# The gate vectors of the second block: two transfers through DRAM in place of products with the identity

## The chip, the cores and the metric

The kernel runs on one core of a Trainium2 chip, as one launch. The metric is the device time in microseconds (us), from the start to the end of the execution. The core has TensorE (PE), VectorE (DVE), ScalarE (ACT), GpSimd (POOL), and SyncE (SP), which here issues most of the DMA transfers, and 16 DMA engines.

## The reference, cut to what matters

Two blocks of two layers each run one after the other on 256 tokens of width 1024. The change concerns the second block only. There each layer has a modulation vector of 6 x 1024 numbers per stream (the latent tokens and the context tokens), and two of the six parts are gates. A gate multiplies, column by column, what a mixer or an MLP gives back, before the sum and the norm:

```python
for i in range(DEPTH):
    mod = (silu_c @ ada_w[i] + ada_b[i])[:, None, :]
    mod_c = silu_cc @ ada_w[i] + ada_b[i]
    sh1, sc1, g1, sh2, sc2, g2 = jnp.split(mod, 6, axis=-1)
    sh1c, sc1c, g1c, sh2c, sc2c, g2c = jnp.split(mod_c, 6, axis=-1)
    h = x * (1.0 + sc1) + sh1
    ...                                  # y = retention (layer 0) or neighbourhood attention (layer 1)
    x = layer_norm_2(DN_ALPHA * x + g1 * y, ln_g[i, 0], ln_b[i, 0])
    h = x * (1.0 + sc2) + sh2
    x = layer_norm_2(DN_ALPHA * x + g2 * sq_relu_mlp(h, mlp_w1[i], mlp_w2[i]), ln_g[i, 1], ln_b[i, 1])
    if not last:
        ctx = layer_norm_2(DN_ALPHA * ctx + g1c * yc, ln_g[i, 0], ln_b[i, 0])
        ...                              # the same MLP for ctx, with g2c
```

So six gate vectors of 1024 numbers are used: g1, g1c, g2, g2c of layer 0, and g1, g2 of layer 1.

## The kernel before

All five engines have programs written out by hand, each in its own order; they meet only at semaphores. `Lane` counts what each engine gives and takes.

**Weights.** SP fetches each weight unit (128 x 2048 numbers, two transfers of 512 KB) into one of four `raw` slots. ACT copies a unit to `w_hi` in a shorter form (L419, two halves), DVE subtracts it from `raw` and leaves the rest in `w_lo` (L426, two halves), and PE makes each product out of three: hi by hi, hi by lo, lo by hi (L444, L445, L446). There are two `w_hi`/`w_lo` slots. ACT may fill a slot again only when PE has begun on the next unit (semaphore `w_used`), so at each new unit of PE the chain is PE, ACT L419, DVE L426, and then PE two units on.

**Stages in time.** The first block ends with its feed-forward layer; its down part takes some 5.5 us of PE a unit and ends at 791 us. A layer norm follows (POOL makes the power -0.5, L1077 and L1080). Then the retention mixer (to 1200 us), the MLP of layer 0 with 512 tokens (`mlp4`, 1235 to 1600 us), the attention mixer (to 1830 us) and the MLP of layer 1 with 256 tokens (`mlp2`, 1844 to 2020 us). After each norm of the second block POOL applies gain and bias to the tokens that are kept (`pool_stream`, L1973 and L1976: products and sums of two tensors in SBUF), while PE already works on the first MLP units.

**Gates.** `mod` holds the modulation with the column number spread over the 128 partitions. The gate is wanted along the free dimension and equal in all partitions (`gate_b`, two streams by 1024). `pe_gates` makes this out of products: for each group of 128 columns the gate's column, repeated 128 times, by the identity, into banks 4 to 7; `act_gates` copies the banks to `gate_b`. It runs at four places: in the down part of the last feed-forward layer of the first block (two streams), behind the first unit of `mlp4` (two), behind the second of the eight query and key units of the attention mixer (one), and behind the first unit of `mlp2` (one). A product on full float32 shows as two records in the trace. DVE reads `gate_b` only at the end of each of the four stages. `up_by_stream` and `up` are PE's units of the up part; from the third unit on they wait for `hh`, that is for DVE's `hh_lo` (L2402).

Of the kernel before, what the change touches and what calls it, by code (L numbers as in the profile page):

```python
# [215 lines left out]
def build(nc, a, out):  # L216

    with ExitStack() as ctx:
# [10 lines left out]

        sb = tensors(ctx)  # L230
# [686 lines left out]
        def pe_ffn(pe, l):  # L917
# [9 lines left out]
            for j in range(FT // 2 - (2 if l + 1 < DEPTH else 1)):  # L927
# [3 lines left out]
                if j == 2:  # L931
                    pe.eng.wait_ge(on("conv_f"), pe.takes("conv_f", 2))
                    if l + 1 == DEPTH:
                        pe.eng.wait_ge(on("coef"), pe.takes("coef"))
                        pe_gates(pe, 0, 2, (0, 1))
                if j == 4 and l + 1 == DEPTH:
                    pe_gates_end(pe, (0, 1))
# [338 lines left out]
        def act_ffn(act, l):  # L1276
# [25 lines left out]
            for n in range(FT // 2):  # L1302
                if n + (2 if l + 1 < DEPTH else 1) < FT // 2:
                    split_hi(act)
                if l + 1 == DEPTH:
                    if n == 3:
                        act.eng.wait_ge(on("coef"), act.takes("coef"))
                        act_gates(act, (0, 1))
# [512 lines left out]
        def pe_gates_end(pe, streams):  # L1821

            pe.eng.wait_ge(on("gate_b"), pe.takes("gate_b", 2 * len(streams)))
# [346 lines left out]
        def dve_head(dve, h, last_head):  # L2170
# [53 lines left out]
            if last_head:  # L2224
                dve.eng.wait_ge(on("y_add"), dve.given("y_add"))
                dve.eng.wait_ge(on("xc_in"), dve.takes("xc_in", 16))
                dve.eng.wait_ge(on("gate_b"), dve.takes("gate_b", 4))
# [83 lines left out]
        def pe_mlp(pe, l, tiles):  # L2311
# [24 lines left out]
            def step(what, b, c):  # L2336
# [4 lines left out]
                for j in range(2):  # L2341
                    if what == "up":
                        if j == 0 and pe.loop is None and c == 0:
# [4 lines left out]
                            pe_gates(pe, l, 5, streams)  # L2348
# [6 lines left out]
                if what == "up" and pe.loop is None and c == 0:  # L2355
                    pe_gates_end(pe, streams)
# [3 lines left out]
        def act_mlp(act, tiles):  # L2360
# [3 lines left out]
            def step(what, b, c):  # L2364
                for j in range(2):
# [12 lines left out]
                    if what == "up" and j == 0 and act.loop is None and c == 0:  # L2378
                        act_gates(act, streams)
# [4 lines left out]
        def dve_mlp(dve, tiles):  # L2384
# [3 lines left out]
            def step(what, b, c):  # L2388
                if c is last_down:
                    return  # L2390
                for j in range(2):
# [13 lines left out]
                    else:  # L2405
# [3 lines left out]
                        if j == 0 and dve.loop is None:  # L2409
                            dve.eng.wait_ge(on("y_add"), dve.given("y_add"))  # L2410
                            dve.eng.wait_ge(on("gate_b"), dve.takes("gate_b", 2 * len(streams)))
# [94 lines left out]
        def pe_nat(pe):  # L2506
# [6 lines left out]
            for f in range(NF):  # L2513
# [5 lines left out]
                if f == 1:  # L2519
                    pe.eng.wait_ge(on("nv"), pe.takes("nv", 4))  # L2520
                    pe_gates(pe, 1, 2, (0,))
            pe_gates_end(pe, (0,))
# [65 lines left out]
        def act_nat(act):  # L2588
# [9 lines left out]
            for f in range(NF):  # L2598
# [5 lines left out]
                if f == 1:  # L2604
                    act_gates(act, (0,))
# [277 lines left out]
```

## Time and profile before

| | |
|---|---|
| Median of 3 runs | 2032.34 us (2031.33 to 2033.85) |
| Profiled execution, its own time | 2037.13 us |
| Its span, first to last instruction | 2035.2 us |
| PE busy | 1971.5 us, 97% of the span |
| DVE busy | 1254.9 us, 62% |
| ACT busy | 864.2 us, 42% |
| POOL busy | 174.4 us, 9% |
| Mean DMA rate | 146 GB/s |
| Mean granted TensorE clock | 0.993 of full speed |

The profiled execution took 4.79 us more than the median of the runs shown, of which 1.93 us lie outside the span. Times in the rows are counted from the start of the span. A row of the timeline is one group of equal instructions: its start, its busy time, engine, line, and in square brackets the idle time of the engine before it and what ended that.

### The profile page before, as it was taken

The page shows a single profiled execution, that of the slowest core. Times are in us where ns is not written, and L with a number is a line of the kernel's source. Part 1 is how long each engine was busy: PE and PEld are TensorE (multiplying, and loading weights), DVE is VectorE, ACT ScalarE, POOL GpSimd, SP SyncE. Part 2 cuts the span into 40 slices and gives each one's busy share as a digit, 9 for nine tenths or more (in the row PEclk, how much of TensorE's full clock was granted, in tenths as well). Part 3 has the DMA queues.
Part 4 walks back from the last instruction along what each step waited for, and adds up shares of the span by engine and source line. Part 5 has one row for each costly group of instructions (what it writes and reads, how often), then busy time and mean ns, then how long its engine had stood idle before and what let it go on. Part 6 is the DMA issues. An engine that isn't in the chain of part 4 may idle for free.

```text
span 2035.2 us, 32477 instructions
## 1 busy us (share of the span) xinstructions
PE 1971.5 (97%) x12673; PEld 1615.6 (79%) x12673; DVE 1254.9 (62%) x2071; ACT 864.2 (42%) x1445; POOL 174.4 (9%) x175
## 2 busy tenths in 40 slices
PE   9998999999899999999999999999999999999997
PEld 8766999797569988777777777888888787667996
DVE  6666787576568856544545477444445833866667
ACT  5442665354336646232222225223222433855442
POOL 2012000001010001000000005000000330303000
PEclk9999999999999999999999999999999999999999
DMA  8489665465977645222322222323323262545662
GB/s 252 166 311 294 182 186 190 145 187 180 339 222 212 193 178 179 83 83 62 95 70 82 70 76 87 100 89 97 100 86 103 84 141 97 86 103 161 201 186 83
DMA packets 327160, 297.25 MB, mean 146 GB/s; under 512 B 35030, under 2 KB 248354, under 8 KB 327056
## 3 DMA queue, kind: packets, MB, share of 16 engines
q1 hardware_dynamic: 322960, 283.22, 46.0%
q0 software_dynamic: 4096, 12.58, 1.9%
q8 instruction: 74, 1.21, 0.2%
q14 instruction: 30, 0.25, 0.0%
HBM read 294.70 MB, written 1.05 MB: 145 GB/s over the span
## 4 chain that ended last, share of the span: by engine, by line
PE 82%; DVE 10%; DMA 3%; ACT 2%; issue 2%; POOL 1%; SPq 1%; DVEq 0%; ACTq 0%; POOLq 0%
PE ps L444 24%; PE ps L446 24%; PE ps L445 24%; DVE w_lo L426 2%; PE ps L2088 2%; DMA raw<-in_ada_w 2%; PE ps L595 1%; DVE npr L2664 1%; PE ps L2533 1%; PE ps L2069 1%; DVE small L1866 1%; PE ps L1817 1%; ACT w_hi L419 1%; PE ps L489 1%; DMA raw<-in_w_in 0%
## 5 line engine op out<-in xcount | busy, mean ns | idle before, releaser
L426 DVE TENSOR_TENSOR w_lo<-raw,w_hi 128x1024 fp32r<-128x1024 f32 x428 | 526.0, 1270 | 333.6 <-ACT w_hi L419 333.3
L419 ACT ACTIVATE w_hi<-raw 128x1024 fp32r<-128x1024 f32 x428 | 428.9, 1052 | 532.0 <-PE ps L444 444.9
L444 PE MATMUL ps<-zt_hi,w_hi 128*128 128x512 f32 (+1 forms) x816 | 275.0, 337 | 5.0 <-issue 1.4
L446 PE MATMUL ps<-zt_hi,w_lo 128*128 128x512 f32 (+1 forms) x816 | 274.1, 336 | 0.0
L445 PE MATMUL ps<-zt_lo,w_hi 128*128 128x512 f32 (+1 forms) x816 | 274.0, 336 | 0.0
L444 PE MATMUL ps<-xt_hi,w_hi 128*128 128x256 f32 x864 | 241.6, 280 | 1.9 <-DVE w_lo L426 1.8
L446 PE MATMUL ps<-xt_hi,w_lo 128*128 128x256 f32 x864 | 241.1, 279 | 0.0
L445 PE MATMUL ps<-xt_lo,w_hi 128*128 128x256 f32 x864 | 241.0, 279 | 0.0
L444 PEld LDWEIGHTS ps<-zt_hi,w_hi 128*128 128x128 f32 x816 | 153.9, 189 | 25.1 <-issue 3.5
L445 PEld LDWEIGHTS ps<-zt_lo,w_hi 128*128 128x128 f32 x816 | 154.1, 189 | 18.3
L446 PEld LDWEIGHTS ps<-zt_hi,w_lo 128*128 128x128 f32 x816 | 154.1, 189 | 18.2
L444 PEld LDWEIGHTS ps<-xt_hi,w_hi 128*128 128x128 f32 x864 | 164.5, 190 | 2.3 <-DVE w_lo L426 2.3
L445 PEld LDWEIGHTS ps<-xt_lo,w_hi 128*128 128x128 f32 x864 | 163.1, 189 | 0.0
L446 PEld LDWEIGHTS ps<-xt_hi,w_lo 128*128 128x128 f32 x864 | 162.9, 189 | 0.0
L444 PE MATMUL ps<-w_hi,hh_hi 128*128 128x512 f32 x384 | 150.8, 393 | 0.8 <-DVE w_lo L426 0.8
L445 PE MATMUL ps<-w_lo,hh_hi 128*128 128x512 f32 x384 | 151.3, 394 | 0.0
L446 PE MATMUL ps<-w_hi,hh_lo 128*128 128x512 f32 x384 | 150.7, 393 | 0.0
L444 PE MATMUL ps<-w_hi,zt_hi 128*128 128x512 f32 x320 | 127.1, 397 | 1.3 <-DVE w_lo L426 1.2
L446 PE MATMUL ps<-w_hi,zt_lo 128*128 128x512 f32 x320 | 126.0, 394 | 0.0
L445 PE MATMUL ps<-w_lo,zt_hi 128*128 128x512 f32 x320 | 125.6, 392 | 0.0
L2000 DVE TENSOR_TENSOR y<-y,ps 128x512 f32<-128x512 f32 x108 | 72.1, 684 | 86.0 <-PE ps L446 86.0
L1694 DVE SCALAR_TENSOR_TENSOR hid<-ps,par,hid 128x254 f32<-128x254 f32 (+1 forms) x176 | 76.8, 478 | 40.2 <-ACT hid L1281 34.2
(388 smaller groups left out, 3322.9 us busy)
## 6 DMA issues: line engine op xcount, KB each, us to landing
raw<-in_mlp_w SPq DMA_DIRECT2D x128, 512.0 KB, 4.4
raw<-in_ada_w SPq DMA_DIRECT2D x96, 512.0 KB, 7.0
raw<-in_w_up SPq DMA_DIRECT2D x88, 512.0 KB, 5.0
raw<-in_w_in SPq DMA_DIRECT2D x56, 512.0 KB, 4.8
raw<-in_ret_w_in SPq DMA_DIRECT2D x48, 512.0 KB, 4.2
raw<-in_w_down SPq DMA_DIRECT2D x44, 512.0 KB, 4.2
raw<-in_nat_w_in SPq DMA_DIRECT2D x24, 512.0 KB, 5.0
raw<-in_w_out SPq DMA_DIRECT2D x16, 512.0 KB, 7.1
```

The lines of the kernel that those rows point to most:

```text
L419: nc.scalar.activation(w_hi[:, t, w], raw[:, s, w], ACT.Copy).then_inc(on("w_hi"), act.gives("w_hi"))
L426: nc.vector.tensor_tensor(w_lo[:, t, w], raw[:, s, w], w_hi[:, t, w].bitcast(F32), ALU.subtract).then_inc(on("w_split"), dve.gives("w_split"))
L444: first = nc.tensor.matmul(out_ap, l_hi, r_hi, start=start, stop=False)
L445: nc.tensor.matmul(out_ap, l_hi, r_lo, start=False, stop=False)
L446: return first, nc.tensor.matmul(out_ap, l_lo, r_hi, start=False, stop=stop)
L489: first = T.matmul(outs[0], w_hi[:, t, k * P:(k + 1) * P], x[:, k, :], start=n == k == 0, stop=False)
L595: ins = T.matmul(ps[5][32 * k:32 * k + 32, :], cs[:, 4 * j + k, 22 - 2 * g:54 - 2 * g], raw[:, s, 512 * k:512 * k + 512], start=g == j == ...
L1694: V.scalar_tensor_tensor(dst[:, d:SEQ], src[:, 0:SEQ - d], w, dst[:, d:SEQ], ALU.mult, ALU.add).then_inc(on(sem), dve.gives(sem))
L1817: ins = T.matmul(ps[4 + 2 * s + k // 4][:, hs(k % 4)], mod[:, l, 8 * chunk + k, s:s + 1].to_broadcast([P, P]), ident, start=True, stop=True)
L1866: V.bn_stats(small[:, o:o + 6], x).then_inc(on("v_step"), dve.gives("v_step"))
L2000: V.tensor_tensor(yt, yt, ps[banks[n]][:, :], ALU.add).then_inc(on("y_add"), dve.gives("y_add"))
L2088: ins = T.matmul(ps[4 + t][:, :], s_, rv[:, v, :], start=n == 0, stop=n == len(keys) - 1)
```

## The change

The products, the copies out of PSUM and the waits that belonged to them are gone at all four places. In their stead GpSimd issues DMAs. At one place in the program, after the context has been fetched and once DVE has given `coef`, it stores the six gate vectors to a scratch in DRAM, `gate_rows` (six transfers, each of 1024 separate numbers of 4 bytes), and waits until they have landed. Later it loads each gate from there with a transfer that gives the same 4096 bytes to all 128 partitions (512 KB into SBUF), two for a stage of two streams and one for a stage of one. DVE's waits for `gate_b` count DMA increments now.

```diff
+        gate_rows = nc.dram_tensor("gate_rows", (4, 2, KT, P), F32, kind="Internal").ap()
...
                     if l + 1 == DEPTH:
                         pe.eng.wait_ge(on("coef"), pe.takes("coef"))
-                        pe_gates(pe, 0, 2, (0, 1))
                 if j == 4 and l + 1 == DEPTH:
-                    pe_gates_end(pe, (0, 1))
                     pe.eng.wait_ge(on("xc0_in"), pe.takes("xc0_in", 16))
...
-        def pe_gates(pe, l, chunk, streams):
-
-            for s in streams:
-                for k in range(KT):
-                    ins = T.matmul(ps[4 + 2 * s + k // 4][:, hs(k % 4)],
-                                   mod[:, l, 8 * chunk + k, s:s + 1].to_broadcast([P, P]), ident, start=True, stop=True)
-                ins.then_inc(on("gate_ps"), pe.gives("gate_ps"))
...
-        def act_gates(act, streams):
-            for s in streams:
-                act.eng.wait_ge(on("gate_ps"), act.takes("gate_ps"))
-                for j in range(2):
-                    act_copy(gate_b[:, s, 512 * j:512 * j + 512], ps[4 + 2 * s + j][:, :]).then_inc(
-                        on("gate_b"), act.gives("gate_b"))
+        GATES = ((0, 2, (0, 1)), (0, 5, (0, 1)), (1, 2, (0,)), (1, 5, (0,)))
+
+        def pool_gate_rows(pool):
+
+            pool.eng.wait_ge(on("coef"), pool.takes("coef"))
+            for n, (l, chunk, streams) in enumerate(GATES):
+                for s in streams:
+                    pool.eng.dma_start(gate_rows[n, s].rearrange("k p -> p k"),
+                                       mod[:, l, 8 * chunk:8 * chunk + KT, s],
+                                       allow_slow_non_contiguous=True).then_inc(
+                                           on("gate_row"), pool.gives("gate_row", 16))
+            pool.eng.wait_ge(on("gate_row"), pool.given("gate_row"))
+
+        def pool_gates(pool, n):
+
+            for s in GATES[n][2]:
+                pool.eng.dma_start(gate_b[:, s, :], gate_rows[n, s].rearrange("k p -> (k p)").partition_broadcast(P)).then_inc(
+                    on("gate_b"), pool.gives("gate_b", 16))
...
-            dve.eng.wait_ge(on("gate_b"), dve.takes("gate_b", 2))
+            dve.eng.wait_ge(on("gate_b"), dve.takes("gate_b", 16))
...
                 if l + 1 == DEPTH:
+                    pool_gate_rows(pool)
                     pool.eng.wait_ge(on("y_ps"), pool.takes("y_ps", 8 * DEPTH - 2))
                     eng.dma_start(xc[:, :, :], a["ctx_2"].rearrange("b (t p) d -> p (b t) d", p=P)).then_inc(
                         on("xc_in"), pool.gives("xc_in", 16))
+                    pool_gates(pool, 0)
                 pool_norm(pool)
...
                 pool_stream(pool, ALL)
+                pool_gates(pool, 1 + m)
             pool_nat(pool)
             pool_powers(pool, LAT)
             pool_gains2(pool, 1, 0)
             pool_stream(pool, LAT)
+            pool_gates(pool, 3)
             pool_gains2(pool, 1, 1)
```

The lines of the changed kernel differ by a few numbers from those of the kernel before (L444 to L446 there are L445 to L447).

PE in `mlp4`, behind the first unit (256 columns wide, by stream), where `hh` is given by DVE L2402. Before:

```order
L444 MATMUL ps<-zt_hi,w_hi 128x256
L445 MATMUL ps<-zt_lo,w_hi 128x256
L446 MATMUL ps<-zt_hi,w_lo 128x256
L1817 MATMUL ps<-cst,mod 128x128 x16
L444 MATMUL ps<-zt_hi,w_hi 128x512 [waits w_split,hh]
L445 MATMUL ps<-zt_lo,w_hi 128x512
```

And after the change:

```order
L445 MATMUL ps<-zt_hi,w_hi 128x256
L446 MATMUL ps<-zt_lo,w_hi 128x256
L447 MATMUL ps<-zt_hi,w_lo 128x256
L445 MATMUL ps<-zt_hi,w_hi 128x512 [waits w_split,hh]
L446 MATMUL ps<-zt_lo,w_hi 128x512
```

The sixteen products are gone, and the second unit stands directly behind the first, with the same waits.

ACT at the same place (L1086 of before is the copy out of the banks, and of `hm` to `hh_hi`). Before:

```order
L2370 ACTIVATE hm<-ps 128x512
L1086 ACTIVATE hh_hi<-hm 128x512 [waits hm] x2
L419 ACTIVATE w_hi<-raw 128x1024 [waits w_used,raw_full0]
L419 ACTIVATE w_hi<-raw 128x1024
L1086 ACTIVATE gate_b<-ps 128x512 [waits gate_ps]
L1086 ACTIVATE gate_b<-ps 128x512
L1086 ACTIVATE gate_b<-ps 128x512 [waits gate_ps]
L1086 ACTIVATE gate_b<-ps 128x512
L2370 ACTIVATE hm<-ps 128x512 [waits hh,up_ps]
```

And after:

```order
L2365 ACTIVATE hm<-ps 128x512
L1085 ACTIVATE hh_hi<-hm 128x512 [waits hm] x2
L420 ACTIVATE w_hi<-raw 128x1024 [waits w_used,raw_full0]
L420 ACTIVATE w_hi<-raw 128x1024
L2365 ACTIVATE hm<-ps 128x512 [waits hh,up_ps]
```

The split of the weights still stands behind the two copies of `hh_hi`; only the four copies behind it went.

POOL around the norm at the end of the first block (L1077 and L1080 of before are L1076 and L1079 after). Before:

```order
L1030 DMA ln_gb<-in_ln_b 128x1024
L2757 DMA xc<-in_ctx 128x2x1024
L2761 DMA xc<-in_ctx 128x2x1024 [waits y_ps]
L1077 TENSOR_SCALAR small<-small 128x1 [waits ssq]
L1080 TENSOR_TENSOR small<-small,cst 128x1 [waits p_step]
```

And after:

```order
L1029 DMA ln_gb<-in_ln_b 128x1024
L2746 DMA xc<-in_ctx 128x2x1024
L1818 DMA gate_rows<-mod 128x8x1 [waits coef]
L1818 DMA gate_rows<-mod 128x8x1 x5
L2751 DMA xc<-in_ctx 128x2x1024 [waits y_ps,gate_row]
L1827 DMA gate_b<-gate_rows 128x1024 x2
L1076 TENSOR_SCALAR small<-small 128x1 [waits ssq]
L1079 TENSOR_TENSOR small<-small,cst 128x1 [waits p_step]
```

Six stores stand behind the first fetch of the context, and two loads of 512 KB stand between the second fetch and the norm's power.

## Rows read from the trace of the kernel before

**Rows 1.** The page, part 1: busy time of PE.

```profile
PE 1971.5 (97%) x12673; PEld 1615.6 (79%) x12673; DVE 1254.9 (62%) x2071; ACT 864.2 (42%) x1445; POOL 174.4 (9%) x175
```

**Rows 2.** Timeline of PE in the down part of the first block.

```profile
742.02 3.73 PE L1817 MATMUL ps<-cst,mod 128*128 128x128 f32 x32
745.51 0.47 PE L444 MATMUL ps<-w_hi,h_hi 128*128 128x512 f32 x1
```

**Rows 3.** Timeline of PE in the query and key units.

```profile
1670.16 1.95 PE L1817 MATMUL ps<-cst,mod 128*128 128x128 f32 x16
1671.86 0.37 PE L444 MATMUL ps<-zt_hi,w_hi 128*128 128x256 f32 x1
```

**Rows 4.** Windows: stretch, its length, busy time by engine, PEclk, DMA share, GB/s.

```profile
613.00:640.00 27.00, 27.00 (x241) 27.00 (x240) 22.76 (x39) 18.85 (x31) 0.00 (x0) 1.00 0.79 213
745.50:791.00 45.50, 45.50 (x210) 37.62 (x209) 22.37 (x22) 25.48 (x38) 0.00 (x0) 1.00 0.51 162
1672.30:1733.70 61.40, 60.53 (x340) 47.88 (x338) 25.20 (x40) 23.02 (x41) 2.61 (x2) 1.00 0.35 106
1264.40:1600.00 335.60, 335.60 (x1456) 272.22 (x1457) 168.62 (x219) 96.19 (x131) 1.61 (x2) 1.00 0.29 91
```

**Rows 5.** Timeline at the norm after the first block.

```profile
791.78 0.72 POOL L2761 DMA_DIRECT2D xc<-in_ctx  x1 [186.83 <-PE ps L446]
...
793.19 2.48 DVE L1612 SCALAR_TENSOR_TENSOR xn<-xs,small,ln_gb 128x1024 f32<-128x1024 f32 x2
...
795.81 1.59 POOL L1080 TENSOR_TENSOR small<-small,cst 128x1 f32<-128x1 f32 x1
...
797.50 1.28 DVE L1621 SCALAR_TENSOR_TENSOR xs<-xn,small,ln_gb 128x1024 f32<-128x1024 f32 x1 [0.51 <-POOL small L1080]
```

**Rows 6.** Timeline at the start of `mlp4`, PE and ACT, then DVE and POOL.

```profile
1248.05 3.73 PE L1817 MATMUL ps<-cst,mod 128*128 128x128 f32 x32
...
1249.60 1.23 ACT L1086 ACTIVATE hh_hi<-hm 128x512 fp32r<-128x512 f32 x2 [0.27 <-DVE hm L2396]
1252.11 2.01 ACT L419 ACTIVATE w_hi<-raw 128x1024 fp32r<-128x1024 f32 x2 [1.29 <-PE ps L444]
...
1253.28 1.98 DVE L426 TENSOR_TENSOR w_lo<-raw,w_hi 128x1024 fp32r<-128x1024 f32 x1 [3.12 <-ACT w_hi L419]
...
1258.53 5.67 DVE L2402 TENSOR_TENSOR hh_lo<-hm,hh_hi 128x512 fp32r<-128x512 f32 x2
...
1251.77 2.41 POOL L1973 TENSOR_TENSOR xs<-y,gn 128x1024 f32<-128x1024 f32 x1
1260.93 2.71 POOL L1976 TENSOR_TENSOR xs<-xs,gn 128x1024 f32<-128x1024 f32 x1
...
1264.32 0.50 PE L444 MATMUL ps<-zt_hi,w_hi 128*128 128x512 f32 x1 [1.34 <-DVE hh_lo L2402]
```

**Rows 7.** Timeline at the start of `mlp2`.

```profile
1850.97 0.75 ACT L1086 ACTIVATE hh_hi<-hm 128x256 fp32r<-128x256 f32 x2 [0.21 <-DVE hm L2396]
1853.24 4.56 DVE L426 TENSOR_TENSOR w_lo<-raw,w_hi 128x1024 fp32r<-128x1024 f32 x2 [1.97 <-ACT w_hi L419]
...
1869.58 0.49 PE L444 MATMUL ps<-w_hi,hh_hi 128*128 128x512 f32 x1 [0.77 <-DVE w_lo L426]
```

**Rows 8.** Windows before, in and after stretches of half clock.

```profile
552.00:556.40 4.40, 1.30 (x14) 0.16 (x8) 3.50 (x12) 1.65 (x8) 0.00 (x0) 0.98 1.05 388
556.50:559.50 3.00, 3.00 (x14) 1.26 (x14) 0.00 (x0) 0.28 (x1) 0.00 (x0) 0.50 1.05 390
...
1235.50:1238.80 3.30, 3.30 (x17) 3.30 (x17) 1.43 (x3) 3.25 (x9) 0.00 (x0) 0.50 0.90 334
1239.00:1242.30 3.30, 3.30 (x31) 3.30 (x30) 2.56 (x2) 2.34 (x3) 1.98 (x1) 1.00 0.21 76
```

**Rows 9.** POOL's DMA issues (line, count, busy us, mean ns), then landing (KB, us).

```profile
L1965 POOL DMA_DIRECT2D gn<-in_ln_b x4 | 2.2, 549 | 0.0
...
lay<-in_w_in POOLq DMA_DIRECT2D x2, 32.0 KB, 6.8
```

More of the change, by code:

```diff
@@ L1307, in act_ffn @@
                         act.eng.wait_ge(on("coef"), act.takes("coef"))
-                        act_gates(act, (0, 1))
                     if n in (5, 7):
@@ L1810, in dve_turned @@
             ins.then_inc(on("zT"), dve.gives("zT"))
-        def pe_gates(pe, l, chunk, streams):
-            for s in streams:
-                for k in range(KT):
-                    ins = T.matmul(ps[4 + 2 * s + k // 4][:, hs(k % 4)],
-                                   mod[:, l, 8 * chunk + k, s:s + 1].to_broadcast([P, P]), ident, start=True, stop=True)
-                ins.then_inc(on("gate_ps"), pe.gives("gate_ps"))
-        def pe_gates_end(pe, streams):
-            pe.eng.wait_ge(on("gate_b"), pe.takes("gate_b", 2 * len(streams)))
-        def act_gates(act, streams):
-            for s in streams:
-                act.eng.wait_ge(on("gate_ps"), act.takes("gate_ps"))
-                for j in range(2):
-                    act_copy(gate_b[:, s, 512 * j:512 * j + 512], ps[4 + 2 * s + j][:, :]).then_inc(
-                        on("gate_b"), act.gives("gate_b"))
+        GATES = ((0, 2, (0, 1)), (0, 5, (0, 1)), (1, 2, (0,)), (1, 5, (0,)))
[12 more added lines that the diff above has]
+                    on("gate_b"), pool.gives("gate_b", 16))
         def half(c):
@@ L2226, in dve_head @@
                 dve.eng.wait_ge(on("xc_in"), dve.takes("xc_in", 16))
-                dve.eng.wait_ge(on("gate_b"), dve.takes("gate_b", 4))
+                dve.eng.wait_ge(on("gate_b"), dve.takes("gate_b", 32))
                 for c in range(2):
@@ L2347, in step @@
                                 up(j)
-                            pe_gates(pe, l, 5, streams)
                         else:
@@ L2354, in step @@
                         down_unit(pe, hh_hi[:, b, :, :], hh_lo[:, b, :, :], tiles, down_banks(j, tiles))
-                if what == "up" and pe.loop is None and c == 0:
-                    pe_gates_end(pe, streams)
             mlp_program(pe, f"mlp{len(tiles)}", step)
@@ L2377, in step @@
                         split_hi(act)
-                    if what == "up" and j == 0 and act.loop is None and c == 0:
-                        act_gates(act, streams)
             mlp_program(act, f"mlp{len(tiles)}", step)
@@ L2410, in step @@
                             dve.eng.wait_ge(on("y_add"), dve.given("y_add"))
-                            dve.eng.wait_ge(on("gate_b"), dve.takes("gate_b", 2 * len(streams)))
+                            dve.eng.wait_ge(on("gate_b"), dve.takes("gate_b", 16 * len(streams)))
                             dve_ahead(dve, 0, tiles)
@@ L2520, in pe_nat @@
                     pe.eng.wait_ge(on("nv"), pe.takes("nv", 4))
-                    pe_gates(pe, 1, 2, (0,))
-            pe_gates_end(pe, (0,))
             release(pe)
@@ L2603, in act_nat @@
                              scale=ND ** -0.5).then_inc(on("n_q"), act.gives("n_q"))
-                if f == 1:
-                    act_gates(act, (0,))
             def exponents(g, hs_):
```

## Prediction

> **What bounds the kernel now.** I read the page's busy times first: PE is busy 97% of the span [rows 1]. With so full an engine the first guess is that every product taken out shortens the kernel by its own time. This must be checked place by place, because a product taken out just ahead of a wait only makes the wait longer. So I went to the timeline of PE at the four places where the gate products run, and asked of each which wait of PE ends last behind it. For the stretches behind them I read the windows, where a PE busy time equal to the stretch's length says that PE never waits.
>
> - Down part of the first block: the products start at 742.02 and the next weight product at 745.51, so they hold PE for 3.49 us [rows 2]. From there to 791 us PE is busy 45.50 of 45.50 us [rows 4]. PE is the bound, and what is taken out moves everything behind it.
> - Query and key units of the attention mixer: 1670.16 to 1671.86, 1.70 us for half as many products [rows 3], and then 60.53 of 61.40 us busy [rows 4]. PE is the bound here too.
> - Start of `mlp4`: PE has 1.34 us of idle time before 1264.32, ended by DVE's `hh_lo` [rows 6]. The last word there is DVE's and not PE's.
> - Start of `mlp2`: PE waits 0.77 us before 1869.58, for DVE's `w_lo` [rows 7]. Again it is DVE.
>
> **The change, part by part.**
>
> *Products in the down part.* Gain 3.49 us, with a slightly slow first product behind them (0.47 us) some 0.1 us more: **-3.6**. DVE is busy 22.37 and ACT 25.48 us of the 45.50 [rows 4], so both have room to follow. The four copies of ACT cost nothing before and give nothing.
>
> *Products in the attention mixer.* 1.70 us and 0.1 in the same way: **-1.8**.
>
> *Products in `mlp4`.* They hold PE from 1248.05, about 3.6 us. After the change the second unit starts at 1248.05 and would end 3.6 us earlier, near 1259.3. What must be followed is the chain to `hh_lo`. ACT's split of the next weights waited for PE's new unit, to 1252.11. Without that wait it stands behind the two copies of `hh_hi`, which end at 1249.60 + 1.23 = 1250.83 [rows 6]. So it moves up by about 1.3 us, and its first half (1.06 us of the 2.01) ends near 1251.9 instead of 1253.2. DVE's `w_lo` could then start at 1251.9. But POOL is in its chain of gain and bias, and the rows show that the two engines do not run such work side by side. POOL's operation of 1251.77 takes 2.41 us, to 1254.18, and the `w_lo` that started at 1253.28 took 1.98 us and ended at 1255.26: 1.08 us after POOL's end. The two `hh_lo`, half as wide, took 5.67 us and end at 1264.20, 0.56 us after POOL's last operation (1260.93 + 2.71 = 1263.64) [rows 6]. Each engine waits for the other's operation and they take turns. A `w_lo` that comes at 1251.9 comes 0.1 us after POOL has begun, and still ends at 1254.18 + 1.08 = 1255.26. All behind it stays on POOL's beat, `hh_lo` ends at 1264.20, and PE goes on at 1264.32 as before. The 3.6 us become idle time, 1.34 + 3.6 = 4.9 us: **0** here. The Trainium skill (GPSIMD Engine Reference, Key points) says that GpSimd shares its SBUF interfaces with VectorE and that instructions with two SBUF inputs contend. The rows above agree; by a reading of the removed products alone the sum would be 3.6 us better.
>
> *The clock behind that gap.* After a stretch in which PE was busy only 1.30 of 4.40 us, the granted clock was 0.50 (1.2 GHz), and it was 0.50 too from 1235.5, behind the norm, where PE also stops for short times. At 0.50 PE ran 17 products in 3.30 us, and in the next 3.30 us, at full clock, 31 of the same kind [rows 8]: 14 products of 0.106 us, so such a stretch costs 1.5 us. With 4.9 us of idle time before 1264.32, longer than any in this trace, I expect one there, and afterwards PE is busy 335.60 of 335.60 us [rows 4], so that nothing makes up for it: **+1.5**, between 0 and 2.5, as the return to full clock comes sooner or later.
>
> *Products in `mlp2`.* They hold PE 1.8 us. The same two steps: ACT's split moves up to the end of `hh_hi`, 1850.97 + 0.75 = 1851.72, from about 1852.07, so 0.35 us. `w_lo` (4.56 us for two that cost 2.4 when POOL is still) is on POOL's beat [rows 7]. The chain of DVE and ACT to the `w_lo` for which PE waits at 1869.58 then starts at the same time: **0**, and at most 1.8.
>
> *Six stores.* `coef` is given at 613 us, and POOL then has nothing to do until 791.78 (it waited 186.83 us [rows 5]). The nearest row is the load of 1024 pieces of 32 bytes, which landed 6.8 us after its issue [rows 9]. Six in a row are 41 us at most, under a cover of 178. What the stores can touch is the weights' transfers. PE is busy 27.00 of 27.00 us there with 241 products [rows 4], so a unit of 48 takes some 5.4 us; four slots are ahead, less the landing of one: some 16 us of cover. **0**, upper bound below, among the rivals.
>
> *Two loads at the norm.* They stand in POOL's queue ahead of the norm's power, for which DVE waits. Each costs 0.55 us to issue [rows 9], so POOL is free 1.1 us later, at 793.6. It then meets DVE's pair of L1612 (793.19 to 795.67) and takes turns with it. Before, the first tile's power was ready when DVE had ended this pair, and L1621 could follow at once. Now the power's second operation comes while the pair's second runs, and is done some 0.5 us after it, an estimate from the turns of rows 6 and the small operation's size; L1621's first starts near 796.3 instead of 795.7. The second tile's power again takes its turn behind that, as before, so DVE's second L1621 moves from 797.50 [rows 5] to 798.1: **+0.6**. Both ends: 0 if the turns fall well, 1.1 plus a turn of DVE (1.28), 2.4, if badly. Behind it PE, ACT, POOL's rope transfer and the exponentials follow in a chain, so it counts in full. The 1 MB that lands then is gone from the DMA engines before that transfer: the context's own 1 MB lands in 8 us.
>
> *Other loads.* They stand behind POOL's work in the program, with more than 150 us to their use, and delay only the next gain transfers and a memset, by 0.55 or 1.1 us under far larger waits: 0.
>
> **Sum.** -3.6 - 1.8 + 0 + 1.5 + 0 + 0 + 0.6 = **-3.3 us**. Against the profiled execution's own 2037.13 us this gives 2033.8. That execution was 4.79 us above the median of the runs, so for a median I take the difference off 2032.34: **2029.0 us**, 0.16% less.
>
> **The rivals.** I count a change of up to 0.2% (4.1 us) as no change, about what a measurement can tell.
>
> 1. *My sum without the clock's part.* The gap before 1264 costs no or little clock. For it: gaps of 1.3 us passed without a loss (the one at 1264.32 itself). Against: rows 8. Then -4.8 us, 2027.5, just over the bound.
> 2. *DVE gets its turn first.* The margin in `mlp4` is 0.1 us: if `w_lo` comes before POOL's operation of 1251.77, it is done at about 1253.0 and POOL's last operations are shifted against it; `hh_lo` then ends about one turn of POOL (2.3 us) earlier. The same holds if the half clock at 1235.5 does not occur and PE is 1.5 us earlier. Then -7.1 us, or -5.6 with a loss of clock: 2025.2 to 2026.7. The far end of this is that all the products pay in full (3.6 + 3.6 + 1.8 + 1.8 - 0.6 = 10.2 us): 2022.1.
> 3. *The norm pays more.* At the bad end of the loads' place (+2.4) and with a half clock in the gaps of PE there as well (1.5), the sum is 0: 2032.3.
> 4. *The stores starve the weights.* This ends on the other side. The stores go in pieces of 4 bytes, far below any piece in the trace. If they take half of the DMA engines for a long time, the weights, whose transfers keep 0.79 of the engines busy in that stage [rows 4], fall behind by (0.79 - 0.5) / 0.79 = 0.37 us for each us. The cover of 16 us is used up after some 43 us, 7 us a store, and from there each 10 us cost 3.7. At 80 us in all it would be +13.7 - 3.3, 2042.7. For it speaks nothing in the rows; against it, that 1024 pieces of 32 bytes landed in 6.8 us. The Trainium skill (DMA: Bandwidth & Descriptors, Specifications) says that pieces under 512 bytes are not moved at full rate and are handled by read-modify-write. No row here shows 4-byte data going to DRAM.
>
> **How the numbers follow.** Forecast 0.40; rival 1 0.15; rival 2 0.27; rival 3 0.10; rival 4 0.08. Faster by over 0.2%: rivals 1 and 2, 0.42. Within 0.2%: the forecast and rival 3, 0.50. Slower: 0.08. For the range I take in rival 2 but for its far end and rival 3: 2023.5 to 2033.0.
>
> **What would show it.** In the changed trace: (a) down part and query and key units without a gap, 3.6 and 1.8 us shorter; (b) L1621's second operation 0.6 us later against the end of the down part; (c) a PE gap of some 4.9 us at the start of `mlp4`, ended by `hh_lo`, while POOL's chain keeps its beat, and the granted clock at 0.50 behind it; (d) the wait in `mlp2` before the first down unit longer by about 1.8 us in all; (e) six stores landed long before 791, PE without gaps from 613 on. A gap in `mlp4` under 3 us, or PE idle in the up part of the first block, would make me wrong.

## The result, and the profile after

| | before | after |
|---|---|---|
| Median (4 runs each) | 2031.84 us (2031.01 to 2033.85) | 2044.40 us (2043.60 to 2045.54) |
| Ratio, 95% interval | | 1.0073 (1.0042 to 1.0104) |
| Profiled execution, its own time | 2037.13 us | 2044.18 us |

The kernel became slower by 12.6 us, outside the forecast range of 2023.5 to 2033.0. What happened is the fourth rival, to which I had given 0.08. The page after, part 1, against [rows 1]:

```profile
PE 1957.4 (96%) x12577; PEld 1601.7 (78%) x12577; DVE 1254.4 (61%) x2071; ACT 858.0 (42%) x1433; POOL 183.0 (9%) x187
```

PE has less to do by 14.1 us and the kernel takes longer. So PE must wait somewhere, and the first thing to look for is its longest idle time. From its timeline:

```profile
630.03 0.28 PE L447 MATMUL ps<-xt_hi,w_lo 128*128 128x256 f32 x1
647.39 0.58 PE L445 MATMUL ps<-xt_hi,w_hi 128*128 128x256 f32 x1 [17.09 <-DVE w_lo L427]
```

It stands in the up part of the first block, where no product was changed. DVE's `w_lo` is named, but DVE waited for ACT and ACT for `raw`: the weights had not come. ACT's timeline:

```profile
645.03 2.00 ACT L420 ACTIVATE w_hi<-raw 128x1024 fp32r<-128x1024 f32 x2 [18.96 <-DMA raw<-in_w_up]
```

The timeline of POOL shows what began shortly before, and the windows what it did to the transfers (length, PE, PEld, DVE, ACT, POOL, PEclk, DMA share, GB/s):

```profile
602.42 5.35 POOL L1818 DMA_DIRECT2D gate_rows<-mod  x6 [8.44 <-DVE coef L1750]
```

```profile
607.00:610.00 3.00, 3.00 (x29) 3.00 (x28) 2.94 (x6) 2.61 (x4) 0.77 (x1) 1.00 2.29 32
610.00:613.00 3.00, 3.00 (x29) 3.00 (x28) 2.00 (x4) 1.45 (x3) 0.00 (x0) 1.00 0.37 1
613.00:616.00 3.00, 3.00 (x29) 3.00 (x28) 2.85 (x6) 2.19 (x4) 0.00 (x0) 1.00 1.07 10
616.00:619.00 3.00, 3.00 (x29) 3.00 (x28) 1.57 (x3) 0.40 (x1) 0.00 (x0) 1.00 1.09 18
...
622.00:630.00 8.00, 6.36 (x54) 6.11 (x54) 4.66 (x8) 1.75 (x4) 0.00 (x0) 1.00 0.70 60
630.00:640.00 10.00, 0.30 (x3) 0.10 (x1) 0.00 (x0) 0.00 (x0) 0.00 (x0) 0.68 0.58 37
640.00:650.00 10.00, 2.61 (x12) 2.61 (x13) 3.74 (x6) 4.97 (x8) 0.00 (x0) 0.50 0.96 222
650.00:660.00 10.00, 10.00 (x87) 10.00 (x87) 7.41 (x13) 4.82 (x9) 0.00 (x0) 0.97 1.10 286
```

From 607 to 640 us almost nothing arrives: 32, 1, 10, 18 GB/s, and later at most 60. The kernel before must be read at the same place of its program and not at the same time: the first product of its up units stands at 605.54 us, here it stands at 594.57, so everything in this stretch lies 11.0 us later there. Its windows at that place, which I had not read:

```profile
618.00:621.00 3.00, 3.00 (x29) 3.00 (x28) 2.96 (x6) 2.59 (x4) 0.00 (x0) 1.00 1.00 280
621.00:624.00 3.00, 3.00 (x29) 3.00 (x29) 2.00 (x4) 1.48 (x3) 0.00 (x0) 1.00 0.47 118
624.00:627.00 3.00, 3.00 (x29) 3.00 (x28) 2.85 (x7) 2.16 (x4) 0.00 (x0) 1.00 1.10 306
627.00:630.00 3.00, 3.00 (x29) 3.00 (x28) 2.42 (x5) 2.04 (x4) 0.00 (x0) 1.00 0.22 57
630.00:633.00 3.00, 3.00 (x29) 3.00 (x28) 2.86 (x5) 1.60 (x3) 0.00 (x0) 1.00 1.10 308
...
622.00:720.00 98.00, 98.00 (x868) 98.00 (x867) 84.01 (x145) 65.58 (x108) 0.00 (x0) 1.00 0.67 193
```

There the weights come in bursts of one unit each, 193 GB/s on average, which is what PE uses up. In the changed kernel the packets of the six stores run from 606.74 to 640.99 us (from the DMA records), and in this time the weights came at 39 GB/s, in its first 12 us at 17.

How far the weights were ahead can be read off the unit for which PE then waited, the seventh of the up units. In the kernel before, SP issued its two transfers at 617.24 and 617.80 us, they had landed at 624.2, and PE began on it at 638.50 (landings from the DMA records). The split takes the last 2.4 us of that (ACT at 645.03 to PE at 647.39 in the rows above), so the unit came 11.9 us before it was needed. In the changed kernel the same place lies 11.0 us earlier, at 613.2; there the unit landed at 645.0, 31.8 us late. 31.8 - 11.9 = 19.9 us, and 1.6 us lost at half clock behind the gap (3.2 us of products at 0.50) make the 21.5 us that will be measured below. The place is not to blame: a refill of the slots does run behind the norm, but 1.9 of its 2 units had come when the stores began (DMA records), and the next six units of the kernel before are only 0.5 to 1.4 us further ahead.

The other places came out nearly as forecast. Against [rows 4], the down part still has no gap:

```profile
742.00:791.00 49.00, 49.00 (x224) 40.46 (x223) 21.92 (x22) 25.86 (x37) 0.00 (x0) 1.00 0.59 193
```

At the norm ([rows 5]), the timelines of POOL and DVE:

```profile
798.99 0.71 POOL L2751 DMA_DIRECT2D xc<-in_ctx  x1 [191.22 <-PE ps L447]
799.69 1.13 POOL L1827 DMA_DIRECT2D gate_b<-gate_rows  x2
800.89 0.56 POOL L1076 TENSOR_SCALAR small<-small 128x1 f32<-128x1 f32 x1
...
800.12 2.48 DVE L1610 SCALAR_TENSOR_TENSOR xn<-xs,small,ln_gb 128x1024 f32<-128x1024 f32 x2
803.13 1.28 DVE L1619 SCALAR_TENSOR_TENSOR xs<-xn,small,ln_gb 128x1024 f32<-128x1024 f32 x1 [0.53 <-POOL small L1079]
804.92 1.28 DVE L1619 SCALAR_TENSOR_TENSOR xs<-xn,small,ln_gb 128x1024 f32<-128x1024 f32 x1 [0.51 <-POOL small L1079]
```

L1619 waits for POOL twice now, where before it waited once. At the start of `mlp4` ([rows 6]) and of `mlp2` ([rows 7]), timelines of DVE, POOL and PE:

```profile
1257.58 4.93 DVE L427 TENSOR_TENSOR w_lo<-raw,w_hi 128x1024 fp32r<-128x1024 f32 x2 [1.72 <-ACT w_hi L420]
1262.44 5.63 DVE L2395 TENSOR_TENSOR hh_lo<-hm,hh_hi 128x512 fp32r<-128x512 f32 x2
...
1267.60 2.72 POOL L1974 TENSOR_TENSOR xs<-xs,gn 128x1024 f32<-128x1024 f32 x1
...
1268.19 0.61 PE L445 MATMUL ps<-zt_hi,w_hi 128*128 128x512 f32 x1 [3.09 <-DVE hh_lo L2395]
...
1874.27 0.50 PE L445 MATMUL ps<-w_hi,hh_hi 128*128 128x512 f32 x1 [1.95 <-DVE w_lo L427]
```

The gaps grew from 1.34 to 3.09 us and from 0.77 to 1.95 us. Behind the first one the clock is at half, 9 products in 3.30 us against 15 in the next 3.30 (windows, as [rows 8]):

```profile
1268.40:1271.70 3.30, 3.30 (x9) 2.53 (x9) 1.59 (x3) 3.00 (x4) 2.98 (x3) 0.50 0.03 10
1271.80:1275.10 3.30, 3.30 (x15) 2.68 (x15) 3.14 (x5) 0.01 (x1) 0.00 (x0) 0.99 0.87 310
```

### The profile page after: what moved, and what is told of

Same layout as the page of the kernel before. It is cut to its first block, busy times and chain, and to the rows that moved or that the text cites. A ratio compares the mean times of both kernels' runs of the same rounds, so it can differ in the third digit from the quotient of the medians.

```text
span 2042.4 us, 32285 instructions
## 1 busy us (share of the span) xinstructions
PE 1957.4 (96%) x12577; PEld 1601.7 (78%) x12577; DVE 1254.4 (61%) x2071; ACT 858.0 (42%) x1433; POOL 183.0 (9%) x187
## 4 chain that ended last, share of the span: by engine, by line
PE 80%; DVE 9%; DMA 5%; ACT 2%; issue 2%; SPq 1%; POOL 1%; DVEq 0%; ACTq 0%; POOLq 0%
PE ps L445 24%; PE ps L446 23%; PE ps L447 23%; DVE w_lo L427 2%; DMA raw<-in_ada_w 2%; PE ps L2086 2%; DMA raw<-in_w_up 2%; PE ps L596 1%; DVE npr L2653 1%; DMA nb<-in_nat_rpb 1%; PE ps L2067 1%; PE ps L2524 1%; ACT w_hi L420 1%; DVE small L1864 1%; SPq L393 0%
## 5 line engine op out<-in xcount | busy, mean ns | idle before, releaser
L445 PE MATMUL ps<-zt_hi,w_hi 128*128 128x512 f32 (+1 forms) x816 | 276.3, 339 | 7.1 <-DVE hh_lo L2395 3.1
L446 PE MATMUL ps<-zt_lo,w_hi 128*128 128x512 f32 (+1 forms) x816 | 275.6, 338 | 0.0
L447 PE MATMUL ps<-zt_hi,w_lo 128*128 128x512 f32 (+1 forms) x816 | 275.4, 337 | 0.0
L445 PE MATMUL ps<-xt_hi,w_hi 128*128 128x256 f32 x864 | 241.1, 279 | 19.3 <-DVE w_lo L427 18.9
L447 PE MATMUL ps<-xt_hi,w_lo 128*128 128x256 f32 x864 | 240.3, 278 | 1.9 <-issue 1.9
L446 PE MATMUL ps<-xt_lo,w_hi 128*128 128x256 f32 x864 | 240.4, 278 | 0.0
L445 PEld LDWEIGHTS ps<-xt_hi,w_hi 128*128 128x128 f32 x864 | 163.7, 189 | 22.1 <-DVE w_lo L427 19.6
L445 PEld LDWEIGHTS ps<-zt_hi,w_hi 128*128 128x128 f32 x816 | 154.6, 189 | 27.6 <-issue 5.2
L447 PEld LDWEIGHTS ps<-zt_hi,w_lo 128*128 128x128 f32 x816 | 155.2, 190 | 18.4
L446 PEld LDWEIGHTS ps<-zt_lo,w_hi 128*128 128x128 f32 x816 | 154.2, 189 | 18.2
L446 PEld LDWEIGHTS ps<-xt_lo,w_hi 128*128 128x128 f32 x864 | 164.0, 190 | 0.0
L447 PEld LDWEIGHTS ps<-xt_hi,w_lo 128*128 128x128 f32 x864 | 163.7, 190 | 0.0
L445 PE MATMUL ps<-w_hi,hh_hi 128*128 128x512 f32 x384 | 151.4, 394 | 2.0 <-DVE w_lo L427 2.0
L446 PE MATMUL ps<-w_lo,hh_hi 128*128 128x512 f32 x384 | 151.6, 395 | 0.0
L447 PE MATMUL ps<-w_hi,hh_lo 128*128 128x512 f32 x384 | 150.1, 391 | 0.0
L445 PE MATMUL ps<-w_hi,zt_hi 128*128 128x512 f32 x320 | 126.5, 395 | 1.2 <-DVE w_lo L427 1.2
L446 PE MATMUL ps<-w_lo,zt_hi 128*128 128x512 f32 x320 | 125.7, 393 | 0.0
L447 PE MATMUL ps<-w_hi,zt_lo 128*128 128x512 f32 x320 | 125.4, 392 | 0.0
```

The source lines that it names most:

```text
L445: first = nc.tensor.matmul(out_ap, l_hi, r_hi, start=start, stop=False)
L446: nc.tensor.matmul(out_ap, l_hi, r_lo, start=False, stop=False)
L447: return first, nc.tensor.matmul(out_ap, l_lo, r_hi, start=False, stop=stop)
```

## The experiments

Medians varied more in these runs than in the first (the kernel before gave 2019 to 2039 us), so I compare mainly the length of parts between fixed products in PE's timelines. The same parts came out equal to some hundredths of a us in many kernels. "Up part": from the first product of the output projection of the first block's last mixer, over the norm (31.65 us together), to the first product of the down part of the feed-forward layer, 151.65 us before. In the kernel as changed it is 173.12 (+21.5).

**1. The stores alone, and the change without them.** `e1` adds only the stores to the kernel before; `e2` is the changed kernel with one store of rows.

```diff
                 if l + 1 == DEPTH:
+                    pool_gate_rows(pool)
                     pool.eng.wait_ge(on("y_ps"), pool.takes("y_ps", 8 * DEPTH - 2))
```

> The kernel before with the six stores of 1024 x 4 bytes added at the changed kernel's place, used by nobody; all products of the gates stay. Theory A (the stores alone cost, and everything else of the change gains): PE has the same gap of some 17 us before the up units near 647 us, ended by the weights' transfer, a half clock behind it, and the kernel takes 18 to 21 us more than before, 2050 to 2053 us; that is more than the 12.6 us of the whole change. Rival B (the loss comes from the stores together with something else of the change): less than 12.6 us more. Rival C (POOL, which waits for the stores, is late for other work): the gap is somewhere else, behind a wait for POOL.

```diff
-            for n, (l, chunk, streams) in enumerate(GATES):
...
+            pool.eng.dma_start(gate_rows.rearrange("n s k p -> (n s k) p"), cst[0:64, 0:P]).then_inc(
+                on("gate_row"), pool.gives("gate_row", 16))
```

> The changed kernel with one store of 64 rows of 512 bytes in place of the six; the rows are of another table, so that the gates have other values and only the time counts. Theory A: no gap of PE between 600 and 700 us, and the rest of the change shows alone: -3.6 (down part), +0.5 (norm), -1.1 (first units of the MLP of 512 tokens), -1.7 (query and key units), +1.5 (half clock behind the gap in that MLP), 0 to -1 at the last MLP; together -4.4 to -5.4 us against before, some 2027 us. My forecast's own sum would say -3.3. Rival B: a loss of several us remains, since the loads cost too: 2032 or more.

`e1`: 2046.5 us, ratio 1.0080 (1.0052 to 1.0108), up part 172.72, and the same gap in PE's timeline:

```profile
646.48 0.58 PE L445 MATMUL ps<-xt_hi,w_hi 128*128 128x256 f32 x1 [16.92 <-DVE w_lo L427]
```

`e2`: up part 151.67, ratio 0.9997 (0.9971 to 1.0023), which is too wide for the small terms. Theory A holds for the place; the medians alone would leave room for rival B's size. The parts of `e2` against undisturbed ones with the products: down part 62.12 to 65.70 (-3.6), end of the down part to the first product behind the norm's long gap 10.37 to 9.87 (+0.5), stage of `mlp4` 374.78 to 372.67 (+2.1), query and key stage 123.92 to 125.72 (-1.8), `mlp2` 178.86 to 178.85 (0). Sum -2.8 us. I had expected -4.4 to -5.4 against the profile before, and against that one the parts do give -4.4: its `mlp4` took 374.31 us, with a half clock of its own at 1235.5.

**2. Three stores and twelve.**

> The kernel before with three of the six stores added, gate products kept. Theory A (each store stops the weights for 5.5 us, the first 16 us are covered by the slots that were fetched ahead): 16.5 us of stop, 0 to 2 us more than before. Rival B (each store costs its share, without a cover): 19 / 2 = 9 to 10 us more.

> The kernel before with twelve stores added (the six twice, the second time into another part of the scratch), gate products kept. Theory A: 66 us of stop less 16 us of cover, 50 us more than before, and up to 3 more for the clock. Rival B (a fixed share for each store): 38 to 42 us more. Rival C (the queue of the stores takes turns with the weights once more of them are in it): under 30 us more.

Three: ratio 1.0029 (0.9994 to 1.0064). The up part took 157.47 us, but most of that is a slower pace of PE (last section); between 620 and 640 us PE was idle for 1.8 us. Twelve: ratio 1.0153 (1.0114 to 1.0193), up part 190.33 us. That is the profiled execution, the slowest of the four; the median is 28.5 us above that of before. In its windows PE gets nothing for 20 us:

```profile
618.00:645.00 27.00, 22.43 (x167) 22.16 (x165) 14.21 (x25) 9.03 (x16) 3.70 (x5) 0.87 0.60 38
645.00:665.00 20.00, 0.00 (x0) 0.00 (x0) 0.81 (x1) 1.90 (x2) 0.00 (x0) 0.53 1.16 35
```

A cover exists: rival B falls at three, though its 38 to 42 us would have fitted the profile of twelve (+38.7), and rival C's "under 30" its median. Theory A's 50 us for twelve was too much, because the weights are not stopped: they go on at some 36 to 39 GB/s. A balance by the DMA records, an estimate: weights missing, in us of PE, less PE's idle time is what was covered. Three stores: 15 us at 48 GB/s where PE uses 193, 11 missing, 1.8 idle. Six: 34 us at 39, 27 missing, 19.3 idle. Twelve: 51 us at 36, 42 missing, 27.2 idle. The cover comes out at some 9, 8 and 15 us, around the 11.9 read above. The rest of the 38.7 us is half clock and the slower pace.

**3. The same stores later.**

```diff
                 pool_stream(pool, ALL)
+                if m == 0:
+                    pool_gate_rows(pool)
```

> The kernel before with the six stores added at another place, behind POOL's gain and bias of the first MLP of the second block (about 1264 us), where the weights keep 0.29 of the DMA engines busy; nobody uses them. Theory A (the price is the weights that do not come, so what matters is how far they are ahead of PE): while the stores run, about 33 us, the weights come at 35 GB/s against 91 that PE uses there; 33 x 56 / 91 is 20 us, less a cover of four full slots (here some 10 us of PE a unit, 30 to 40 us): no gap, 0 to 1 us more than before. Rival B (the stores have a price wherever they stand): 15 us or more.

Ratio 0.9998 (0.9978 to 1.0018). In its windows the rate falls as before, and PE does not notice:

```profile
1252.00:1262.00 10.00, 10.00 (x44) 8.06 (x43) 7.63 (x9) 2.32 (x4) 4.81 (x6) 1.00 0.54 5
1262.00:1272.00 10.00, 10.00 (x44) 8.05 (x44) 4.43 (x6) 3.16 (x5) 0.00 (x0) 1.00 0.71 24
1272.00:1285.00 13.00, 13.00 (x59) 10.64 (x58) 7.94 (x11) 5.92 (x8) 0.00 (x0) 1.00 0.76 58
```

Theory A holds: the stores have no price of their own, only that of the weights that do not come in time. Here 36.7 us at 28 GB/s, where PE uses 91, left 25 us of weights missing, and all of it was covered, since a unit lasts PE some 11 us here instead of 5.4. Four units less landing and split, counted as above, would be a lead of some 35 us, an estimate.

**4. What about the stores blocks the engines.** Each kernel adds six transfers of 1024 pieces to the kernel before, at the change's place; only this statement and its scratch differ (here 4 bytes, 64 apart; the last dimension of the scratch is 8, 4 or 1 for the others):

```diff
+        probe = nc.dram_tensor("probe", (6, KT, P, 16), F32, kind="Internal").ap()
...
+                pool.eng.dma_start(probe[n, :, :, 0:1].rearrange("k p c -> p k c"), cst[:, 0:KT].rearrange("p (k c) -> p k c", c=1),
+                                   allow_slow_non_contiguous=True).then_inc(on("gate_row"), pool.gives("gate_row", 16))
```

> The kernel before with six loads of 1024 separate pieces of 4 bytes, from DRAM into SBUF, at the place where the changed kernel stores; nobody uses them. If the size of the pieces alone makes the price: the weights get 35 GB/s for some 33 us and the up part grows by 21 us, as with the stores. If the price is that of writing such pieces to DRAM: up part longer by at most 2 us.

> The kernel before with six stores of 1024 pieces of 32 bytes into a scratch in DRAM in which a gap follows each piece; nobody uses them. If the price goes by the number of pieces written to DRAM below 512 bytes: up part longer by 21 us, as with 4 bytes. If it goes by pieces below 32 bytes alone: at most 2 us.

> The kernel before with six stores of 1024 pieces of 4 bytes, as many as in the change, but each piece 64 bytes from the next in the scratch; nobody uses them. If the price comes from pieces of 4 bytes as such: the weights come at some 35 GB/s for 33 us and the up part is 172.7 us long instead of 151.65. If it comes from pieces that lie side by side in the same 64 bytes of DRAM and are written at the same time: 151.65 to 153 us, as with the 32-byte pieces that lay apart.

> The kernel before with six stores of 1024 pieces of 32 bytes that lie side by side in the scratch without a gap (in the first runs they lay 64 bytes apart); nobody uses them. If neighbours in the same 64 bytes make the price: some of it is here too, two pieces meet instead of sixteen, up part 2 us or more longer than 151.65. If pieces of 4 bytes as such make it: 151.65 to 153 us.

> The kernel before with six stores of 1024 pieces of 4 bytes, each 32 bytes from the next, so that two lie in the same 64 bytes; nobody uses them. Side by side they took 33 us of DMA time, 64 bytes apart 11 us. If the price comes from any two pieces of one 64-byte stretch: clearly over 11 us. If only from more than two: 11 us, and no change of the up part.

> The same with pieces 16 bytes apart, four in the same 64 bytes. If each piece that finds its 64 bytes taken waits for the one before it: between the run with two and the one with sixteen, 15 to 30 us; if the number of neighbours does not matter once there is one: as with two.

> The partner of the runs with pieces 16, 32 and 64 bytes apart: the same six stores out of the same table, whose eight numbers lie side by side in a partition, but into a scratch without gaps; nobody uses them. The change's own stores read numbers that lie 8 bytes apart in SBUF, so that source and target differ between the two. If the target makes the price: 33 us of DMA time and an up part of some 172.7 us. If the source does: 11 us and 151.65 to 153 us.

The middle columns are from the DMA records: the time from the first to the last packet of the six, and the rate of the weights in the 12 us from the first packet. With nothing added, the weights come at 192 GB/s in the same 12 us of the kernel before.

| six transfers of 1024 pieces | first to last | weights | up part |
|---|---|---|---|
| the change's stores, in `e1` (4 bytes, side by side) | 34.1 us | 16 GB/s | 172.72 us |
| 4 bytes side by side, `e16` | 35.1 us | 16 GB/s | 171.72 us |
| 4 bytes, 16 apart, `e15` | 14.8 us | 75 GB/s | 151.65 us |
| 4 bytes, 32 apart, `e14` | 12.7 us | 76 GB/s | 153.02 us |
| 4 bytes, 64 apart, `e10` | 11.0 us | 120 GB/s | 151.63 us |
| 32 bytes, 64 apart, `e8` | 5.9 us | 188 GB/s | 151.65 us |
| 32 bytes side by side, `e11` | 5.2 us | 184 GB/s | 157.64 us (slower pace, no gap) |
| loads of 4 bytes, `e7` | 7.1 us | 182 GB/s | 156.27 us (slower pace, no gap) |

The windows from the first packet on, of `e16` and then of `e10` (all transfers, so a little above the table):

```profile
610.90:622.90 12.00, 11.99 (x107) 11.87 (x106) 9.42 (x17) 7.29 (x12) 0.84 (x1) 1.00 1.26 19
622.90:646.00 23.10, 12.28 (x91) 11.96 (x90) 6.76 (x13) 4.66 (x8) 0.00 (x0) 0.86 0.82 54
```

```profile
609.30:621.30 12.00, 12.00 (x108) 12.00 (x107) 10.08 (x18) 8.26 (x15) 0.90 (x2) 1.00 1.10 124
621.30:624.30 3.00, 3.00 (x29) 3.00 (x29) 2.85 (x6) 1.76 (x4) 0.00 (x0) 1.00 1.06 272
```

In `e10` the weights are back at 272 GB/s 12 us after the first packet. `e16` has the ratio 1.0105 (1.0073 to 1.0137) and the same count, size and source as `e10`, so it is the spacing in DRAM that costs; the source in SBUF does not, since `e1` and `e16` agree. The six runs below them in the table have ratios from 0.9983 to 1.0005, none clear of 1, and PE has no idle time in their up units. What their up parts have above 151.65 also occurs with no store there: 153.03 to 153.05 in `e5`, `e9` and `e12` (3.4 us at half clock at its start, as in `e14`) and 156.28 in `e13` (the slower pace, as in `e7`; `e11` has both). So only pieces of 4 bytes side by side starve PE. With gaps between them they still slow the weights (75 to 120 GB/s), but for too short a time to use up the lead. Stores of 32 bytes and loads of 4 leave the weights nearly their rate. The price falls as fewer pieces share a stretch of 64 bytes, but not in proportion: the step from sixteen pieces to four is by far the largest, and four took 14.8 us where I had expected 15 to 30. At 32 bytes side by side nothing of it is left, so that not any two neighbours do. One rival is not separated: with the spacing the whole target grows too, from 4 KB for each store to 16, 32 and 64 KB, so that the small target and not the shared 64 bytes could be the cause (`e11` fills 32 KB). `e8` also writes its pieces in another order. Why the memory side reacts so was not seen.

**5. Stores in rows.** PE turns the modulation (two transposes), ACT copies 96 rows, POOL stores rows of 512 bytes and loads the first gates at once.

```diff
+                        for m in range(DEPTH):
+                            ins = T.transpose(ps[4][0:96, hs(m)], mod[:, m, :, :].rearrange("p c s -> p (c s)"), ident)
...
+                pool.eng.dma_start(gate_rows[n].rearrange("k s p -> (k s) p"),
+                                   gate_b[16 * chunk:16 * chunk + 16, 0, l * P:l * P + P]).then_inc(
```

> The changed kernel with stores in pieces of 512 bytes: PE turns the modulation of both layers by two transposes in the down part, ACT copies the two tiles of 96 rows, and POOL stores 16 rows of 512 bytes for each of the four places, four stores; the first gates are loaded at once and not at the norm. Theory A (the size of the pieces is what costs): no gap of PE in the up part, the down part 3.3 us shorter than before instead of 3.6, norm 0 instead of +0.5, and the rest as in the kernel with one store of rows: 4 to 6 us less than before. Rival B (any store there costs, or POOL's place in the down part does): not faster than before.

> Gates of the two mixers by rows of 512 bytes through DRAM, as in the kernel with four row stores (two stores now); gates of the two MLPs by the products and copies of the kernel before. Theory A (in the MLPs the products stand in a wait for POOL and DVE and are free, and without them the longer wait costs a half clock): down part 62.4 us instead of 65.7, norm unchanged, stage of the first MLP 372.7 us instead of 374.5 without products, query and key units 1.8 us shorter: 5.1 us less than before and 2 less than with rows alone. Rival B (the products of the MLPs cost their own time): 5.4 us more than with rows alone.

`e6`: up part 151.65, down part 62.36, norm 9.87 again, stage of `mlp4` 374.54; ratio 0.9995 (0.9978 to 1.0012). Its stores land in a few us (POOL's timeline):

```profile
738.38 1.94 POOL L1824 DMA_DIRECT2D gate_rows<-gate_b  x4 [145.86 <-ACT gate_b L1089]
744.50 1.84 POOL L1832 DMA_DIRECT2D gate_b<-gate_rows  x2 [4.17 <-DMA gate_rows<-gate_b]
```

`e9`: down part 62.34, `mlp4` 370.80 (1.9 of the difference is PE's pace, the rest the half clock that is gone), ratio 0.9989 (0.9966 to 1.0011). Theory A holds in both for the up part, the down part, the norm and `mlp4`. It missed the query and key stage, where 123.9 us were expected and both took 126.76: the stage began with 6.8 us of half clock, 14 products in 6.10 us in `e6` where `e2` has 27, which cost more than the products taken out. `mlp2` took 180.44 and 181.39 us instead of 178.85. So the forecast savings of 4 to 6 us do not show even in the sum of the parts, and neither kernel was measurably faster than the one before.

```profile
1592.70:1598.80 6.10, 6.10 (x14) 4.84 (x15) 4.48 (x5) 4.92 (x10) 2.13 (x1) 0.50 0.92 276
```

**6. The wait in `mlp4`.** POOL's gain and bias on 8 columns instead of 1024, without the gate products (`e12`, on `e6`) and with them (`e13`, on the kernel before).

```diff
+                w = slice(0, 8 if len(tiles) == 4 and not pool.thin else D)
-                G.tensor_tensor(x_of(t), y[:, t, :], gn2[:, 0, :], ALU.mult).then_inc(
+                G.tensor_tensor(x_of(t)[:, w], y[:, t, w], gn2[:, 0, w], ALU.mult).then_inc(
```

> The kernel with four row stores, but POOL's gain and bias in the first MLP of the second block works on 8 columns instead of 1024 (what the kept tokens are then worth is changed). Theory A (the first unit's end waits for DVE, and DVE for POOL): from the first product of that MLP to the unit behind the wait 22.4 us instead of 26.9, no gap over 1 us there and no half clock behind it, the rest of the stage 345.8 instead of 347.7: 6 us less than with rows alone. Rival B (DVE and ACT alone make the wait): a gap of 3 us or more stays.

> The kernel before, but POOL's gain and bias in the first MLP of the second block works on 8 columns instead of 1024 (what the kept tokens are then worth is changed). It is the partner of the run with row stores and narrow POOL work, whose stage of that MLP took 365.95 us. Theory A (without POOL's work PE is the bound there, and the products cost their own time): 365.95 + 3.6 = 369.5 us. Rival B (another wait takes POOL's place and covers the products): 366 to 367 us.

`e12`: ratio 0.9950 (0.9928 to 0.9973), no gap, and DVE's pairs at their own pace (timeline):

```profile
1239.91 2.36 DVE L427 TENSOR_TENSOR w_lo<-raw,w_hi 128x1024 fp32r<-128x1024 f32 x2 [1.72 <-ACT w_hi L420]
1242.19 1.28 DVE L2403 TENSOR_TENSOR hh_lo<-hm,hh_hi 128x512 fp32r<-128x512 f32 x2
```

2.36 and 1.28 us, where the changed kernel has 4.93 and 5.63. From the first product of `mlp4` to its first down unit: 44.57 us in `e12` and 48.56 in `e13`, so the products cost 4.0 us there (3.6 forecast). The whole stage took 365.94 and 371.84 us; the second is over the 369.5 forecast, and 1.9 of the difference lies behind the first down unit, where no product differs. With POOL at full work it is 49.39 us with the products (`e1`) and 51.92 without (`e6`): taking them out loses 2.5. `e13` has the ratio 0.9973 (0.9936 to 1.0011).

## Why the prediction was wrong, step by step

- **Six stores, 0: this step failed.** My lines held "41 us at most" of stores against "some 16 us of cover", and the term was put at 0 all the same, with no reason but that 1024 pieces of 32 bytes had landed in 6.8 us. It measured +21.5 us. The time of the stores was right (5.7 us each, bound 6.8). What was wrong is the overlap: pieces of 4 bytes written side by side took the weights from 193 GB/s down to 39 for 34 us, and pieces of 32 bytes do not (`e8`, `e11`), so that row was none for this case. The cover was wrong too, but less: 11.9 us instead of 16, because the last transfers took 6.9 us from the first issue to land and the split 2.4. With 16 us of cover the stores would still have cost some 16 us.
- **Rival 4** had the mechanism, with a chance that was too small and terms that offset each other: "half of the DMA engines" (in truth four fifths of what PE uses were missing) and a cover that was too long. By its own sum a store of 5.7 us would have cost nothing. The Trainium skill (DMA: Bandwidth & Descriptors, Rules for kernel authors) says that a last dimension that is not contiguous becomes one descriptor an element, and that one should rearrange it. The rearranged form was indeed free (`e2` at the same place, `e6` later), but so were `e7` and `e10`, which also move single elements, so the rule alone does not give the price. Nor does the one on pieces under 512 bytes, which I weighed: 32-byte pieces cost nothing here.
- **Products in the down part, -3.6:** 65.70 to 62.12, -3.6. Right. **Query and key units, -1.8:** -1.7 after, -1.8 in `e2`. Right; in `e6` and `e9` a half clock at the start of the stage took it back.
- **Products in `mlp4`, 0:** first product to the end of the gap 26.9 us with the products and without, shown by `e1`, `e2` and `e6`; that POOL sets the beat is shown by `e12`, and the price under it by `e13`. The gap was 4.62 us in `e2` (4.9 forecast) and 3.09 in the changed kernel, whose first unit ran into a half clock and used 1.5 us of it.
- **Half clock behind that gap, +1.5:** there in the changed kernel; +2.1 for the stage in `e2`, +1.0 in the changed kernel. Right within its bounds.
- **`mlp2`, 0:** 178.86 against 178.85 in `e2`. Right. In the changed kernel it took 181.40, by the slower pace: 867 products in 134 us behind its gap, 878 in the kernel before. **Two loads at the norm, +0.6:** +0.5, and 0 with the loads moved ahead (`e6`).

My sum without the stores was -3.3 and `e2`'s parts give -2.8. With the stores the parts of the changed kernel give 21.5 - 3.6 + 0.5 + 1.0 - 1.7 + 2.5 = 20.2 us; the medians say 12.6, between 8.5 and 21.1 by the interval. The stages that are left out scatter by as much as the difference (last section); which of them closes it stays open.

## What to carry to other kernels

Where a transfer is added beside a stream of weights, ask what it does to the others' rate, not only when it lands. Set the time for which that rate is down against the lead of the stream at that place, and take the lead from the trace: landing of one unit to its first use, less the work in between. Compare two traces at the same place of the program, not at the same time. Give pieces of 4 bytes a contiguous form first (the transposes cost 0.2 us of the down part here, 62.36 against 62.12), or put them where the consumer is slow. Products in a wait that other engines set were free here, and taking them out cost clock.

## What the hardware showed unexpectedly

- 6144 pieces of 4 bytes written side by side to DRAM held the weights at 17 GB/s for 12 us and at 39 over 34 us, where 193 are usual; 64 bytes apart they took 11 us. Meanwhile single 512-byte packets of the weights, 0.03 us each otherwise, took 2.2 us on average between 3 and 6 us after the first packet of the stores (DMA records).
- PE runs the same products at two paces without a change of the granted clock: 267 products in 30 us in `e8`, 257 in `e11` and `e7` (windows, the same part of the program). This alone makes the up part 156.3 us instead of 151.65. The program ahead of the up part is the same in all kernels and took from 560.6 to 573.9 us in the profiles, so the medians scatter by more than the small terms. The cause of the two paces is open.

```profile
660.00:690.00 30.00, 30.00 (x267) 30.00 (x266) 25.62 (x45) 19.98 (x33) 0.00 (x0) 1.00 0.66 183
```

```profile
660.00:690.00 30.00, 30.00 (x257) 30.00 (x256) 24.50 (x43) 19.93 (x33) 0.00 (x0) 1.00 0.67 182
```
